# Streamed matmul operands in rows of 256 elements for the 256-token phases, and MLP activation rows 288 elements apart

## The reference

```python
def first_block(...):                       # 256 tokens
    h = h + hybrid_mixer(rmsnorm(h, ...))   # Mamba-2 SSD and gated linear attention, merged, w_o
    h = h + mem_cross_attention(...)        # 4 heads over a memory of 256 tokens
    h = h + swiglu(...)                     # 1024 -> 2 x 2816 -> 1024
    return rmsnorm(h, norm_final)

def second_block(...):                      # 16 meta tokens + 256 tokens = 272
    # layer 0: stick-breaking attention (qkv, w_o), then sq_relu_mlp (1024 -> 4096 -> 1024)
    # layer 1: RG-LRU mixer (w_in, conv, gates, scan, w_out), then sq_relu_mlp
    return rms_norm(h, ...)[:, N_META:]     # the meta tokens are dropped
```

## Time and profile before

| | us |
|---|---|
| runs | 1186.51, 1186.91, 1187.21 |
| median | 1186.91 |
| span of the profiled execution, first to last instruction | 1184.5 |
| around the span (median minus span) | 2.4 |
| TensorE busy | 1172.2 (99%) |
| DVE busy | 840.4 (71%) |
| ACT busy | 679.1 (57%) |

### The profile page before, as it was taken

How to read it: one execution, slowest core, us unless ns; L and a number is a source line. 1 busy time by engine, 2 the same in 40 slices (tenths; PEclk the granted TensorE clock), 3 DMA queues, 4 the chain that set the end, 5 groups by cost and what they waited for, 6 DMA issues and landing times.

```text
span 1184.5 us, 25284 instructions
## 1 busy us (share of the span) xinstructions
PE 1172.2 (99%) x9596; PEld 1150.8 (97%) x9596; DVE 840.4 (71%) x1257; ACT 679.1 (57%) x1029; POOL 38.1 (3%) x60
## 2 busy tenths in 40 slices
PE   8999999999999999999999999999999999999997
PEld 8999899999999999999999999999999999999997
DVE  7998767987856877776677748666545898776453
ACT  6755547656535666655556637556444777665442
POOL 2002311100000000000000000000000000000000
PEclk9999999999999999999999999999999999999999
DMA  6655434576553565565553326556665545666661
GB/s 225 195 175 164 127 108 141 181 216 189 161 163 120 167 196 191 180 189 183 178 147 120 118 73 206 177 175 185 193 182 167 160 144 170 203 184 189 180 191 56
DMA packets 56776, 197.52 MB, mean 167 GB/s; under 512 B 7153, under 2 KB 9457, under 8 KB 56577
## 3 DMA queue, kind: packets, MB, share of 16 engines
q1 hardware_dynamic: 54480, 193.68, 53.2%
q10 hardware_dynamic: 2224, 2.84, 0.8%
HBM read 195.45 MB, written 1.05 MB: 166 GB/s over the span
## 4 chain that ended last, share of the span: by engine, by line
PE 96%; DVE 2%; ACT 1%; issue 1%; DMA 0%; DVEq 0%; SPq 0%; ACTq 0%
PE acc L458 17%; PE acc L459 17%; PE acc L464 17%; PE acc L452 11%; PE acc L454 11%; PE acc L453 11%; PE acc L517 1%; PE acc L518 1%; PE acc L521 1%; PE mix L791 1%; PE mix L772 1%; PE mix L860 1%; DVE wlo L1637 1%; PE mix L660 1%; ACT whi L1130 1%; PE mix L896 1%
## 5 line engine op out<-in xcount | busy, mean ns | idle before, releaser
L1637 DVE TENSOR_TENSOR wlo<-raw,whi 128x1024 fp32r<-128x1024 f32 x366 | 448.0, 1227 | 182.5 <-ACT whi L1130 182.5
L1130 ACT ACTIVATE whi<-raw 128x1024 fp32r<-128x1024 f32 x366 | 385.2, 1057 | 333.0 <-PE acc L464 170.0
L458 PE MATMUL acc<-xh,whi 128*128 128x256 f32 (+1 forms) x1448 | 362.1, 287 | 0.0
L459 PE MATMUL acc<-xl,whi 128*128 128x256 f32 (+1 forms) x1448 | 357.2, 284 | 0.0
L458 PEld LDWEIGHTS acc<-xh,whi 128*128 128x128 f32 x1448 | 272.4, 188 | 4.3 <-issue 3.5
L459 PEld LDWEIGHTS acc<-xl,whi 128*128 128x128 f32 x1448 | 272.9, 188 | 0.3
L464 PE MATMUL acc<-xh,wlo 128*128 128x256 f32 (+1 forms) x1448 | 203.2, 282 | 0.0
L453 PE MATMUL acc<-hl,whi 128*128 128x256 f32 (+1 forms) x688 | 195.4, 284 | 0.0
L452 PE MATMUL acc<-hh,whi 128*128 128x256 f32 (+1 forms) x688 | 195.0, 283 | 0.0
L454 PE MATMUL acc<-hh,wlo 128*128 128x256 f32 (+1 forms) x688 | 194.7, 283 | 0.0
L464 PEld LDWEIGHTS acc<-xh,wlo 128*128 128x128 f32 x1448 | 186.5, 189 | 0.0
(11 more groups left out here) (399 smaller groups left out, 1574.0 us busy)
## 6 DMA issues: line engine op xcount, KB each, us to landing
raw<-w SPq DMA_DIRECT2D x366, 512.0 KB, 3.6
hT<-xT SPq DMA_DIRECT2D x2, 512.0 KB, 6.2
mem<-memT ACTq DMA_DIRECT2D x1, 1024.0 KB, 5.7
rgw<-w ACTq DMA_DIRECT2D x2, 512.0 KB, 5.8
out<-hT SPq DMA_DIRECT2D x4, 128.0 KB, 2.4
out<-hT ACTq DMA_DIRECT2D x4, 128.0 KB, 2.7
xdt<-wsmall SPq DMA_DIRECT2D x1, 192.0 KB, 7.0
pr<-par ACTq DMA_DIRECT2D x1, 114.0 KB, 4.3
```

What stands on the lines that cost most here:

```text
L458: nc.tensor.matmul(dst, whi[:, slot, n, :], rh, start=first, stop=False)
L459: nc.tensor.matmul(dst, whi[:, slot, n, :], rl, start=False, stop=False)
L1130: act.activation(whi[:, j, :, :].rearrange("p k c -> p (k c)"), raw[:, j, :], ACT.Copy)\
L1637: dve.tensor_tensor(wlo[:, j, :, :].rearrange("p k c -> p (k c)"), raw[:, j, :], whi[:, j, :, :].rearrange("p k c -> p (k c)").bitcast(F32 ...
```

## The change

It declares `hh` and `hl` with rows 288 elements apart (1152 bytes), and it adds views on `xh`, `xl`, `yh`, `yl`, `hh` and `hl` that see the same memory as rows 256 elements apart (1024 bytes), block behind block without a gap. Every use with 256 tokens, on TensorE, ACT, DVE and GpSimd, takes the view; every use with 272 tokens, and the gate projection, keeps the declared tile. The reserved room `below` grows with `hh` and `hl`. No instruction, wait or DMA is added, removed or moved.

```diff
-        hh = sb("hh", [P, MLP_KB, T2], F32R, stack=s3)
-        hl = sb("hl", [P, MLP_KB, T2], F32R, stack=s3)
+        hh = sb("hh", [P, MLP_KB, 288], F32R, stack=s3)
+        hl = sb("hl", [P, MLP_KB, 288], F32R, stack=s3)
...
-        sb("below", [P, 4480], stack=s5)
+        sb("below", [P, 5376], stack=s5)
...
+        def packed(tile):
+
+            n = tile.shape[1] * T1
+            return tile[:, :, :].rearrange("p a b -> p (a b)")[:, 0:n].rearrange("p (a b) -> p a b", b=T1)
+
+        xh1, xl1, yh1, yl1, hh1, hl1 = [packed(tile) for tile in (xh, xl, yh, yl, hh, hl)]
+
+        def operands(T):
+            return (xh1, xl1) if T == T1 else (xh, xl)
+
+        def hidden(T):
+            return (hh1, hl1) if T == T1 else (hh, hl)
...
-            unit("xbc", 0, 0, xh, xl, T1, ready=(xl_ready, 0))
+            unit("xbc", 0, 0, xh1, xl1, T1, ready=(xl_ready, 0))
...
-                            token_pair(phase, n - 1, xh, xl, tiles1)
+                            token_pair(phase, n - 1, xh1, xl1, tiles1)
...
-            project("ups", yh, yl, T1, (yl_ready, 0))
-            project("upg", xh, xl, T1, (yl_ready, 8))
-            project("wo", yh, yl, T1, (yl_ready, 16))
+            project("ups", yh1, yl1, T1, (yl_ready, 0))
+            project("upg", xh1, xl1, T1, (yl_ready, 8))
+            project("wo", yh1, yl1, T1, (yl_ready, 16))
...
-            project("xq", xh, xl, T1, operand("xattn"), statistics=lambda: stream_stats("xattn", T1))
+            project("xq", xh1, xl1, T1, operand("xattn"), statistics=lambda: stream_stats("xattn", T1))
...
-                    last = products(acc[:, m % 4, 0:T1], (u0 + b // 8) % 4, b % 8, hh[:, k, 0:T1], hl[:, k, 0:T1],
+                    last = products(acc[:, m % 4, 0:T1], (u0 + b // 8) % 4, b % 8, hh1[:, k, 0:T1], hl1[:, k, 0:T1],
...
-                project(f"up{n}", xh, xl, T, operand(f"mlp{n}"),
+                project(f"up{n}", *operands(T), T, operand(f"mlp{n}"),
...
-                    last = products(acc[:, m, 0:T], (u0 + k // 8) % 4, k % 8, hh[:, k, 0:T], hl[:, k, 0:T],
+                    last = products(acc[:, m, 0:T], (u0 + k // 8) % 4, k % 8, hidden(T)[0][:, k, 0:T], hidden(T)[1][:, k, 0:T],
...
-                act.activation(blk(xh, b, 0, T), blk(hT, b, T2 - T, T2), ACT.Copy,
+                act.activation(blk(operands(T)[0], b, 0, T), blk(hT, b, T2 - T, T2), ACT.Copy,
```

More of the change, by code:

```diff
@@ L571, in small_products @@
                 for k in range(KB):
-                    nc.tensor.matmul(dst[0:48, 0:T1], wsh[:, k, :], xh[:, k, 0:T1], start=k == 0, stop=False)
-                    nc.tensor.matmul(dst[0:48, 0:T1], wsh[:, k, :], xl[:, k, 0:T1], start=False, stop=False)
-                    last = nc.tensor.matmul(dst[0:48, 0:T1], wsl[:, k, :], xh[:, k, 0:T1], start=False,
+                    nc.tensor.matmul(dst[0:48, 0:T1], wsh[:, k, :], xh1[:, k, 0:T1], start=k == 0, stop=False)
+                    nc.tensor.matmul(dst[0:48, 0:T1], wsh[:, k, :], xl1[:, k, 0:T1], start=False, stop=False)
+                    last = nc.tensor.matmul(dst[0:48, 0:T1], wsl[:, k, :], xh1[:, k, 0:T1], start=False,
                                             stop=k == KB - 1)
@@ L683, in _ @@
                 nc.tensor.matmul(mix[:, 2, 0:P], mean1024[:, :], mean1024[:, :], start=True, stop=True)
-            unit("xbc", 0, 0, xh, xl, T1, ready=(xl_ready, 0))
+            unit("xbc", 0, 0, xh1, xl1, T1, ready=(xl_ready, 0))
             pe.wait_ge(hi_ready, 2)
             for k in range(KB):
-                nc.tensor.matmul(acc[:, 1, 0:T1], whi[:, 1, k, :], xh[:, k, 0:T1], start=k == 0, stop=False)
-                nc.tensor.matmul(acc[:, 1, 0:T1], whi[:, 1, k, :], xl[:, k, 0:T1], start=False, stop=False)
+                nc.tensor.matmul(acc[:, 1, 0:T1], whi[:, 1, k, :], xh1[:, k, 0:T1], start=k == 0, stop=False)
+                nc.tensor.matmul(acc[:, 1, 0:T1], whi[:, 1, k, :], xl1[:, k, 0:T1], start=False, stop=False)
             pe.wait_ge(lo_ready, 2)
             for k in range(KB):
-                last = nc.tensor.matmul(acc[:, 1, 0:T1], wlo[:, 1, k, :], xh[:, k, 0:T1], start=False, stop=k == KB - 1)
+                last = nc.tensor.matmul(acc[:, 1, 0:T1], wlo[:, 1, k, :], xh1[:, k, 0:T1], start=False, stop=k == KB - 1)
             last.then_inc(unit_done, 1)
@@ L700, in _ @@
                         if n % 2:
-                            token_pair(phase, n - 1, xh, xl, tiles1)
+                            token_pair(phase, n - 1, xh1, xl1, tiles1)
                     elif m > 1:
-                        unit(phase, n, n % 4, xh, xl, T1)
+                        unit(phase, n, n % 4, xh1, xl1, T1)
                     if m == 3:
@@ L825, in ffn_down @@
                         last.then_inc(unit_done, 1)
-            project("ffi", xh, xl, T1, operand("ffn"), statistics=lambda: stream_stats("ffn", T1))
+            project("ffi", xh1, xl1, T1, operand("ffn"), statistics=lambda: stream_stats("ffn", T1))
             for m in range(KB):
@@ L1109, in _ @@
                         pe.wait_ge(yl_ready, 40 + k + 1)
-                        last = products(acc[:, m, 0:T1], (u0 + m) % 4, k, yh[:, k, 0:T1], yl[:, k, 0:T1],
+                        last = products(acc[:, m, 0:T1], (u0 + m) % 4, k, yh1[:, k, 0:T1], yl1[:, k, 0:T1],
                                         False, k == KB - 1)
@@ L1114, in _ @@
             for m in range(4, KB):
-                unit("lo", m, m % 4, yh, yl, T1)
+                unit("lo", m, m % 4, yh1, yl1, T1)
             mlp(1, T1)
@@ L1399, in swiglu @@
                     act.wait_ge(hid_ready, 4 * i + (j + 1))
-                    act.activation(blk(hh, 2 * i + j // 2, 0, T1), t4[:, j, 0:T1], ACT.Copy).then_inc(hh_ready, 1)
+                    act.activation(blk(hh1, 2 * i + j // 2, 0, T1), t4[:, j, 0:T1], ACT.Copy).then_inc(hh_ready, 1)
             units_loop("ffi", swiglu)
```

42 lines of the change are left out of this document (21 added, 21 removed).

## The result

The changed kernel takes 1192.36 us (median of 5 runs, 1192.09 to 1193.40) against 1186.58 us before (5 runs, 1186.51 to 1187.21): a ratio of 1.0048, 95% interval 1.0037 to 1.0059. It is slower by 5.8 us where 9.3 us less were forecast. The time lies outside the range, and beside the 1191.4 us of the second rival. The change is small, 0.5%, but the interval excludes 1.

A forecast was written before the change was run, and what follows sets the result against it. TensorE, busy 99% of the 1184.5 us span, was taken as the bound, paced by streamed-row layout. Terms 6.4 + 2.9 + 0.2 - 0.2 = 9.3 us less gave 1177.6 us, range 1175.6 to 1185.2 (0.80).

The forecast's parts named there:

- the second rival: Streams collide: packed `xh`/`yh` rows share the weights' place modulo 512 in every matmul, 1.8 ns each; 1191.4 us, chance 0.09.
- rows 5 to 7: Timeline before: a unit takes 2.800 us on `memh`, 2.837 on `xh`, 2.853 on `hh`, 256 columns each.
- the first term: Packed streamed tiles of the 256-token phases: 172 units go from 2.837 to 2.800 us, 6.4 us less.
- rows 12: Three-in-a-row unit on `xh` before: first four blocks take 1.40 us, last four 1.43; used against collision.
- the first rival: Only an exact copy of `memh`'s layout gains, so only `hh`: 1184.0 us, chance 0.14; half the `xh` gain 1180.8, 0.08.
- hh and hl: FFN and second MLP down projections, packed: 54 units go from 2.853 to 2.800 us, 2.9 us less.
- dn0: 272-token down projection, rows 288 apart: 0.2 us less; bounds 1.5 us gain and 0.5 us loss.
- "v": Token pairs with `xh` as weight operand, 8 units: lose 0.2 us if they take the pace of "xv".
- rows 11: Timeline before: 24 matmuls take 2.84 us in "xv", with `memh` as weights, against 2.82 in "v".
- Writers, waits, clock: Other accesses to these tiles: no instruction or wait changes, rows stay contiguous, priced at nothing; granted clock 2.4 GHz throughout.
- The two rules of the Trainium skill: 16-byte cachelines and independent SBUF read ports: by the first the change gives 0; prediction held measured paces against both.
- the cover: ACT and DVE must still split the next weights while units get 1.3% shorter; otherwise units wait for `wlo`.

The follow-up runs named there:

- the sweeps: Changed kernel with each phase's packed views shifted by different byte offsets: 1183.57 and 1184.89 us, then finer offsets 1183.63 us.
- "ups" at 448: Phase "ups" in the changed kernel with a different view offset per phase, here 448 bytes; that kernel took 1184.89 us.
- all six kernels with one place for all phases: Changed kernel, all 256-token rows equally far past weight blocks: 192 (1173.92; weights moved 1172.76; `dn0` too 1179.78), 112 (1163.94), 144 (1183.80), 80 (1189.14 us).
- the kernel with 112: Changed kernel with all 256-token streamed rows, and `dn0` with rows 320 elements apart, 112 bytes past a weight block: 1163.94 us, ratio 0.9803.
- the kernel with 192 and the weights moved: Changed kernel with 256-token rows 192 bytes past a weight block, plus 64 unused bytes ahead of `whi`, moving every tile: 1172.76 us.
- the kernel with place 192: Changed kernel with every streamed row of the 256-token phases 192 bytes past a weight block modulo 256: 1173.92 us, ratio 0.989.

## Why the prediction was wrong

*What bounds the kernel*: right. TensorE has 96% of the chain before and after, and 84 to 97% in the other kernels; the pace of its matmuls can be read off the timeline, and it decides the time. The reading of three paces from rows 5 to 7 was right as well, and so was the view that the layout makes them.

*The step that failed* is the first term, "172 units x (2.837 - 2.800) = 6.4 us", taken as a gain. It came out at 6.4 us more. It took the pace of `memh` for that of any packed row. `memh` differs from the `xh` of before in two things: its rows keep one place, and that place is 32. The term priced the first alone; the packed `xh` keeps place 0. The runs show that the place decides; 0 gave 120.0 in all phases seen, 32 gave 116.7 or 117.8. The second rival named this cause, with a price of 1.8 ns a matmul, measured 120.0 - 118.2 = 1.8, and a total of 1191.4 against 1192.4. It had 0.09. What held it down was the 1.40 us of rows 12, read as "the fast pace exactly", with the first block at place 0. Those four blocks come just after a change of form, at places 0, 64, 128 and 192 in turn, and the next four, at the same places, took 1.43. Only a run of blocks at one place shows what the place is worth; four blocks at four places were too thin for the weight they carried. So was the second ground against the rival, that even the worst stretch of the trace pays 120.0 only in some blocks: no stretch of before held `xh` at place 0, as the first rival itself notes, so the trace could not show what a constant place 0 costs.

*hh and hl*: right in mechanism, half in size: predicted 2.9 us less, 1.35 in the changed kernel. Alone it brings 2.7 us. What the term left out is that the pace of these rows depends on what else the kernel does; with the views of `xh` and `yh` added, the same rows ran at 117.8 and not at 116.7.

*dn0*: taken at 0.2 less, measured 0.0 (96.09 us before and after from first to last matmul). The prediction expected a small gain from two places in turn, and there is none. Its bound of 1.5 us is what rows 1280 bytes apart brought at places 192 and 112, but by chance, as said above; 144 gave 124.4 and 80 gave 125.0 ns.

*"v"*: 0.2 more predicted, 0.45 measured; the sign from rows 11 was right, but half a pair at place 0 takes 2.88 us and not xv's 2.84.

*Writers, waits, clock*: priced at nothing, and nothing shows. In the changed kernel the cover was never tested, since its units got longer; at 113.3 ns it begins to tear, with the 1.4 us in "ups".

*The range*: with `dn0` at its bound of 1.5 us in place of 0.2 the sum gives 1176.3, not the 1175.8 that stands there; it changes nothing in the outcome.

*The two rules of the Trainium skill.* Cachelines of 16 bytes (the Trainium skill's page "SBUF — State Buffer", section Specifications (TRN2)) cannot account for paces from 113.3 to 120.0 at rows of one length that all start on a multiple of 16 bytes; by that rule alone the sweeps would have been flat in all steps of 16. The independence of TensorE's two read ports (the Trainium skill's page "SBUF — State Buffer", section "Who interferes with whom") would leave no room for the distance to count, and the last run does not agree with that: with the rows where they were and the weights moved by 32 bytes, the stream slowed from 113.3 to 118.3 and 119.9. Here the measurement decides.

*What stays open*: why the distance counts, why its effect repeats with 256 bytes, and what selects among the paces of a place. Shown is when the choice falls: a stretch without interruption keeps its pace, "ups" at 448 changed it at a stop of 0.16 us, and in all six kernels with one place for all phases "ffo" has the pace of "ffi" and `dn1` that of `up1`, which they follow without a stop. What it is about an entry that selects the pace is not shown. The pace of the phase ahead is not all of it: "xk", whose rows no run moved against the weights, has 117.8 in the kernel with 112, behind "wo" at 113.3, and 116.7 in the kernel with 192 and the weights moved, behind "wo" at 113.3 as well.

## What to carry to other kernels

When matmuls with a weight load each run back to back, read their start distances over whole units from the timeline, and compare places as well as pitches: how far a streamed row begins past the weight block, modulo 256 bytes, was worth up to 7 ns in 120 here. A pitch that is a multiple of 256 bytes makes every matmul sit at one place, good or bad, so choose the pitch and the offset together and measure the offset; a pitch that wanders ran between good and bad here, at 118.2 and 118.9. Take more than one execution, since a place can have more than one pace. When one phase serves as the model for another, list all in which they differ before pricing one of them.

## What the runs showed of the hardware

- A matmul of 256 columns with its weight load has several constant paces at a granted clock of 0.996 to 0.998, among them 113.3, 116.7, 117.8, 118.3, 118.7, 120.0 ns (at 2.4 GHz the first, second and last of these are 272, 280 and 288 cycles).
- The distance from the weight block to the streamed row modulo 256 bytes decides which of them occur; five pairs of offsets 256 apart agreed to 0.1 ns and a sixth shared one of its two paces, and 32 bytes changed 113.3 to 118.3 or 120.0.
- At one place two paces can occur, in different phases and within one phase on either side of a stop: 117.9 and 113.3 ns around 0.16 us in "ups" at 448. The executions of the kernel with place 192 ran from 1172.45 to 1182.5 us, those with place 112 from 1163.60 to 1164.16.
- Used as the weight operand, the place of a row counts too: the matmuls of "v" were 117.5 ns apart at wandering places, 120.0 at 0 and at 112, and 113.3 in the first two pairs at 192.
